# Second layer's modulation vector: computed by VectorE multiplies and short column sums in the dense rows instead of wide TensorE products before them

## The reference, cut to what matters

```
modulation(cvec, w_ada, b_ada) = split(silu(cvec) @ w_ada + b_ada, 6)      # w_ada[l] is 1024 x 6144
h = rmsnorm(x, norm1_g) * (1 + sc1) + sh1;  x = x + g1 * mixer(h)
h = rmsnorm(x, norm2_g) * (1 + sc2) + sh2;  x = x + g2 * channel(h)
```

## Time and profile before

| | |
|---|---|
| median of 3 runs | 1482.9 us (1482.24 to 1485.37) |
| the profiled execution | 1484.85 us, its span 1483.0 us |
| mean granted TensorE clock | 0.974 of full |
| busy: PE / PEld / DVE / ACT | 1384.1 / 821.8 / 525.7 / 398.7 us |
| chain that ended last, by engine | PE 77%, DMA 12%, DVE 6% |

### The profile page before, as it was taken

The page is one execution under the profiler, slowest core; times in us unless marked ns, Lnnn a source line. Parts: engine busy times, 40 slices in busy tenths (PEclk is TensorE's granted clock), DMA queues, the critical chain, the costliest instruction groups (busy, mean ns, idle before and its releaser), DMA issues.

```text
span 1483.0 us, 25756 instructions
## 1 busy us (share of the span) xinstructions
PE 1384.1 (93%) x11327; PEld 821.8 (55%) x11327; DVE 525.7 (35%) x954; ACT 398.7 (27%) x701; POOL 4.1 (0%) x8
## 2 busy tenths in 40 slices
PE   6899889999999999989898999999999998889886
PEld 3688657888888888878675343333333332223221
DVE  2799884523232333469864112011100010001022
ACT  3522485422222322376482111010110010000001
POOL 0000000000000000000000000000000000000010
PEclk9999899999999999999999999999999999999898
DMA  9997903532331052411418999999999999999995
GB/s 353 385 343 274 352 2 114 171 114 68 103 114 57 29 187 97 143 57 58 171 41 341 399 371 409 406 409 406 409 407 408 408 406 410 405 410 406 408 410 221
DMA packets 147031, 395.92 MB, mean 267 GB/s; under 512 B 7488, under 2 KB 38752, under 8 KB 146912
## 3 DMA queue, kind: packets, MB, share of 16 engines
q1 hardware_dynamic: 144000, 388.86, 68.7%
q10 hardware_dynamic: 2336, 3.24, 0.6%
q0 software_dynamic: 576, 2.10, 0.4%
HBM read 390.76 MB, written 3.41 MB: 266 GB/s over the span
## 4 chain that ended last, share of the span: by engine, by line
PE 77%; DMA 12%; DVE 6%; SPq 2%; ACT 2%; issue 1%; DVEq 0%; ACTq 0%
PE bank L1196 22%; DMA weight_ring<-in_exp_w 9%; PE bank L1154 8%; PE bank L1013 5%; PE bank L1014 5%; PE bank L1012 5%; PE bank L735 4%; PE bank L736 4%; PE bank L737 4%; DMA weight_ring<-in_w_ada 3%; PE bank L1021 3%; PE bank L1022 3%; PE bank L1023 3%; PE bank L1162 2%; PE bank L681 2%; DVE weight_ring L1865 2%
## 5 line engine op out<-in xcount | busy, mean ns | idle before, releaser
L1196 PE MATMUL bank<-weight_ring,gathered 128*32 128x512 f32 (+1 forms) x3840 | 402.2, 569 | 32.9 <-DMA weight_ring<-in_exp_w 27.1
L1196 PEld LDWEIGHTS bank<-weight_ring,gathered 128*32 128x32 f32 x3840 | 127.0, 112 | 283.0 <-issue 282.3
L2259 DVE TENSOR_TENSOR scratch<-scratch,bank 64x512 f32<-64x512 f32 (+1 forms) x60 | 38.4, 640 | 357.2 <-ACT scratch L1672 354.9
L1154 PE MATMUL bank<-weight_ring,scratch 128*32 128x512 f32 x1344 | 157.8, 593 | 2.2 <-DMA weight_ring<-in_exp_w 2.2
L1014 PE MATMUL bank<-slot_halves,slot_halves 128*128 128x512 f32 x336 | 130.9, 390 | 0.0
L1013 PE MATMUL bank<-hT_halves,slot_halves 128*128 128x512 f32 x336 | 130.9, 390 | 0.0
L1012 PE MATMUL bank<-slot_halves 128*128 128x512 f32 x320 | 124.8, 390 | 0.0
L1865 DVE SCALAR_TENSOR_TENSOR weight_ring<-scratch,conv_weights,weight_ring 128x512 f32<-128x512 f32 (+1 forms) x207 | 121.3, 637 | 2.6 <-ACT weight_ring L1453 0.7
L736 PE MATMUL bank<-hT_halves,slot_halves 128*128 128x512 f32 (+1 forms) x352 | 122.0, 347 | 0.0
L735 PE MATMUL bank<-slot_halves,slot_halves 128*128 128x512 f32 (+1 forms) x284 | 105.6, 372 | 8.1 <-DVE slot_halves L1772 5.2
L1154 PEld LDWEIGHTS bank<-weight_ring,scratch 128*32 128x32 f32 x1344 | 43.8, 110 | 100.3 <-issue 91.0
(11 more groups left out here) (303 smaller groups left out, 1576.1 us busy)
## 6 DMA issues: line engine op xcount, KB each, us to landing
weight_ring<-in_exp_w SPq DMA_DIRECT2D x216, 1024.0 KB, 18.5
weight_ring<-in_w_ada SPq DMA_DIRECT2D x24, 2048.0 KB, 13.5
weight_ring<-in_exp_w SPq DMA_DIRECT2D x64, 768.0 KB, 15.0
weight_ring<-in_ffn_w SPq DMA_DIRECT2D x33, 1024.0 KB, 5.4
weight_ring<-in_w_in SPq DMA_DIRECT2D x8, 1024.0 KB, 11.6
weight_ring<-in_w_out SPq DMA_DIRECT2D x4, 2048.0 KB, 11.2
weight_ring<-in_w_in SPq DMA_DIRECT2D x2, 3072.0 KB, 15.2
expert_rows<-scratch ACTq DMA_DIRECT2D x14, 128.0 KB, 6.0
```

Source lines behind the costliest of these rows:

```text
L1154: i = mm(bank[6][quarter, :], at01[:, c0:c0 + BLOCK], w2[:, i_, half * 512:(half + 1) * 512], start=(first and i_ == 0), stop=(last and i_ ...
L1196: i = mm(ps[BLOCK * job:BLOCK * (job + 1), 0:cw], gathered_block(e, k, b), w[:, kk, a * cw:(a + 1) * cw], start=(k == 0), stop=(k == KT - 1))
```

## The change

Layer 1's twelve pieces leave the walk. `modulate`, `turn_modulation`, `modulation_rows` and `modulation` for l = 1 go, and so do their 12 loads of 2 MB. Instead, from dense row 2 on, VectorE multiplies: each weight row k of a piece is scaled with the silu value of its partition and added into an accumulator of 128 x 512. A step is one such instruction; a piece of b = 0 has 16 (8 weight rows for two vectors), the others 8 (the latent vector alone), 128 steps in all. Eight steps go into each of rows 2 to 17, four behind each `piece_rest`. The weights come in halves of 1 MB into two buffers, 24 transfers on SP's queue, placed ahead of the loads of later weight groups. Two rows after a piece's last step, TensorE sums its accumulators over the partitions at the start of a row (`late_sums`): 8 matmuls for a piece of b = 0 and 4 for the others, of the form of L830. `late_modulation` adds the bias.

```diff
-MOD_PIECES = [(l, b, n) for l, b in MOD_TURNS for n in ([0, 3, 1, 2] if (l, b) == (1, 0) else range(4))]
+MOD_TURNS = [(0, 0), (0, 1), (0, 2)]
+MOD_PIECES = [(l, b, n) for l, b in MOD_TURNS for n in range(4)]
+LATE_PIECES = [(b, n) for b in range(3) for n in range(4)]
+LATE_ROW = 2
+        def late_place(piece, v):
+            return 2 * (piece % 2) + v if LATE_PIECES[piece][0] == 0 else piece % 4
+            def late_weights(i):
+                piece, half = divmod(i, 2)
+                b, n = LATE_PIECES[piece]
+                if i == 0:
+                    sp.wait_ge(L[0]["wo_mm"], KT)
+                if i >= 2:
+                    sp.wait_ge(late_step, STEPS_OF_HALF[i - 2])
+                sp.dma_start(late_w[i % 2], k_major(t["w_ada"][1], 512 * (4 * b + n), 512 * (4 * b + n + 1))[
+                    :, 4 * half:4 * half + 4, :]).then_inc(late_landed[i % 2], 16)
+            def late_sums(piece):
+                b, n = LATE_PIECES[piece]
+                pe.wait_ge(late_step, STEPS_OF_PIECE[piece])
+                for j in range(4):
+                    for v in range(2 if b == 0 else 1):
+                        at = 4 * (4 * n + j) + 2 * v
+                        i = mm(bank[LATE_BANK[b]][:, at:at + 2], late_acc[late_place(piece, v)][:, j * P:(j + 1) * P],
+                               const("ones")[:, 0:2], start=True, stop=True)
+                i.then_inc(mod_mm, 1)
-                    if l == 0 and i_ == 5:
-                        modulate(1, 2, 3)
-                        modulate(1, 1, 0)
-                        modulate(1, 1, 1)
...
-                if l == 0:
-                    modulate(1, 0, 0)
-                if l == 0:
-                    modulate(1, 0, 3)
                 norm_broadcast(3 * l + 3, TQ)
-                if l == 0:
-                    modulate(1, 0, 1)
-                    modulate(1, 0, 2)
-                        if n == 3:
-                            turn_modulation(1, 0)
                         if n >= 2:
                             pe.wait_ge(a_ready, n - 1)
+                        for done in range(len(LATE_PIECES)):
+                            if late_row_of(STEPS_OF_PIECE[done] - 1) + 2 == n:
+                                late_sums(done)
+            def late_steps_done(begin, end):
+                for s in range(begin, min(end, len(LATE_STEPS))):
+                    piece, half, k, v = LATE_STEPS[s]
+                    i = 2 * piece + half
+                    if s == 0 or LATE_STEPS[s - 1][0:2] != (piece, half):
+                        dve.wait_ge(late_landed[i % 2], 16 * (i // 2 + 1))
+                    if k == 0:
+                        held_by_piece = [q for q in range(piece) if late_place(q, 0) // 2 == late_place(piece, 0) // 2 or
+                                         LATE_PIECES[q][0] and late_place(q, 0) == late_place(piece, v)]
+                        if held_by_piece:
+                            dve.wait_ge(mod_mm, len(MOD_PIECES) + held_by_piece[-1] + 1)
+                        ts(dst, w, x, None, ALU.mult).then_inc(late_step, 1)
+                    else:
+                        dve.wait_ge(late_step, LATE_STEPS.index((piece, (k - 1) // 4, k - 1, v)) + 1)
+                        stt(out=dst, in0=w, scalar=x, in1=dst, op0=ALU.mult, op1=ALU.add).then_inc(late_step, 1)
                         if 0 < n < NF - 1:
                             piece_rest(2 * n + 2)
+                            if s >= 0:
+                                late_steps_done(s, s + 4)
...
                             piece_rest(2 * n + 3)
+                            if s >= 0:
+                                late_steps_done(s + 4, s + 8)
```

More of the change, by code:

```diff
@@ L36 @@
 RING = TAIL + 6 * D
-MOE0 = 56
+MOE0 = 44
 STAGE = SLOTS - 1
@@ L76, with late_steps, late_row_of @@
 SELECTS = len(GATHERS) + 1
+def late_steps():
+    steps = []
+    for piece, (b, n) in enumerate(LATE_PIECES):
+        for half in range(2):
+            for v in range(2 if b == 0 else 1):
+                for k in range(4):
+                    steps.append((piece, half, 4 * half + k, v))
+    order = []
+    for piece in range(len(LATE_PIECES)):
+        for half in range(2):
+            mine = [s for s in steps if s[0] == piece and s[1] == half]
+            order += sorted(mine, key=lambda s: (s[2], s[3]))
+    return order
+LATE_STEPS = late_steps()
+STEPS_OF_PIECE = [sum(s[0] <= piece for s in LATE_STEPS) for piece in range(len(LATE_PIECES))]
+STEPS_OF_HALF = [sum((s[0], s[1]) <= (i // 2, i % 2) for s in LATE_STEPS) for i in range(2 * len(LATE_PIECES))]
+def late_row_of(step):
+    return LATE_ROW + step // 8
 def unit_at(v):
@@ L261, in backbone @@
         mrow = [ring[:, OFF[2] + 4096 + i * 512:OFF[2] + 4608 + i * 512] for i in range(2)]
+        late_in = [ring[:, OFF[3] + 4096:OFF[3] + 6144], ring[:, TAIL + 4096:TAIL + 6144]]
+        late_w = [a.rearrange("p (k n) -> p k n", k=4) for a in late_in]
+        late_acc = [ring[:, OFF[2] + 4096 + i * 512:OFF[2] + 4608 + i * 512] for i in range(4)]
         conv_sq = [scr[:, 3584 + i * 512:4096 + i * 512] for i in range(NC)]
@@ L276, in backbone @@
                  "o_ready",
-                 "wo_mm", "x1", "sq2", "scaled2", "h2_ready"]
-        once = {n: sem(n) for n in ["norm_mm", "norm_inv", "norm_spread", "ks_mm", "ks_ready", "v_mm", "v_ready", "conv3", "mean_mm",
+                 "wo_mm", "x1", "scaled2", "h2_ready"]
+        once = {n: sem(n) for n in ["sq1", "sq2", "norm_mm", "norm_inv", "norm_spread", "ks_mm", "ks_ready", "v_mm", "v_ready", "conv3", "mean_mm",
                                  "u_sig", "sc_mm", "nb_ready", "pv_mm", "mix_ready", "qk_norm", "qk_rot", "cd_ready", "cd_mm",
@@ L311, in backbone @@
         eps_ready = sem("eps_ready")
+        late_landed = [sem(f"late_weights_{i}") for i in range(2)]
+        late_step = sem("late_step")
         def k_major(w, a, b):
@@ L360, in backbone @@
             ada(0, 2, n, [4, 2, 3][n % 3])
-        for n in range(8):
-            ada(1, 1 + n // 4, n % 4, [2, 3, 4][n % 3])
-            if n == 3:
-                out_projection(0, 0, 0)
+        out_projection(0, 0, 0)
         out_projection(0, 1, 1)
[L366 to L369, removed]
         F[0]["w13"] = [fill([(KT, 256, 0, k_major(t["ffn_w1"][0], 256 * g, 256 * g + 256)),
@@ L399, in backbone, with late_free_row, fill_free_row @@
             last[sl] = n
+        def late_free_row(i):
+            return late_row_of(STEPS_OF_HALF[i - 2] - 1) + 0.9 if i >= 2 else 0
+        def fill_free_row(group):
+            return 2 * (group - STAGE) + 2 if group >= STAGE else -1
         unit_base = [level[s] if s < SLOTS and third == 0 else 0 for s, third in RING_AT]
@@ L516, in fill_sums @@
             return sums(g - 1, 2 - spot % 2)
+        DONE_BEFORE = 3
+        LATE_BANK = [5, 6, 7] if (0, 0) in LATE_PIECES else [None, 4, 7]
+        def late_place(piece, v):
+            return 2 * (piece % 2) + v if LATE_PIECES[piece][0] == 0 else piece % 4
         FIRST_FILL_BANK = [7, 6, 5, 3]
@@ L557, in _ @@
             sp.dma_start(xtok[:, 2:4, :], t["ctx"][0].rearrange("(n p) d -> p n d", p=P)).then_inc(ctx_in, 16)
+            def late_weights(i):
[7 more added lines that the diff above has]
+                    :, 4 * half:4 * half + 4, :]).then_inc(late_landed[i % 2], 16)
+            late = iter(range(2 * len(LATE_PIECES)))
+            waiting = next(late)
             for n, (parts, free) in enumerate(fills):
+                group = (F[0]["w13"] + F[0]["w2"]).index(n) if n in F[0]["w13"] + F[0]["w2"] else None
+                while group is not None and waiting is not None and late_free_row(waiting) <= fill_free_row(group):
+                    late_weights(waiting)
+                    waiting = next(late, None)
                 if n >= SLOTS:
@@ L691, in turn_modulation, with norm_stat @@
                 i.then_inc(mod_t, 1)
-            def norm_stat(sq, src, k, T):
-                pe.wait_ge(sq, k + 1)
+            def norm_stat(sq, src, k, T, squares=0):
+                pe.wait_ge(sq, squares + k + 1)
                 for b in range(T // P):
@@ L881, in _ @@
                 if l == 0:
-                    pe.wait_ge(mod_row, 8)
+                    pe.wait_ge(mod_row, 6)
                 def score(p):
@@ L903, in _ @@
                         if l == 0:
-                            pe.wait_ge(mod_done, 5)
+                            pe.wait_ge(mod_done, 3)
                         else:
@@ L1535, in _ @@
                         modulation_rows(0, 2)
[L1536 to L1539, removed]
                     if l == 1:
@@ L1610, in _ @@
                 if l == 0:
[L1611 removed]
+                    act.wait_ge(mod_mm, 4 * 3)
                 shift(m, l, 1, "scaled2", "h2_ready")
@@ L1793, in modulation, with late_modulation, modulated @@
                 dve.wait_ge(mod_t, turn + 1)
+                ps = bank[7][:, :].rearrange("p (m q) -> p m q", q=32)[:, :, 0:2]
```

(27 more changed lines are left out.)

33 lines of the change are left out of this document (9 added, 24 removed).

## The result

The changed kernel takes 1496.33 us (median of 6 runs, 1494.52 to 1499.7), the kernel before 1482.87 (6 runs); the ratio is 1.0085, 95% interval 1.0074 to 1.0096, so 11.0 to 14.2 us slower. The prediction was 1493.9 us (+11.0), range 1487 to 1500. The profiled execution took 1494.66 us, its span is 1492.9. `rotate` is now L869, the taps L1937, the first score reduction L2024, a step of VectorE L1875 or L1878, `piece_rest` L1824, `late_sums` L774, `norm_broadcast` L763, the rows L1059 to L1061.

A forecast was written before the change was run, and what follows sets the result against it. TensorE was taken as full in walk and dense rows, VectorE nearly full in the walk. Terms -2.9 (walk), -1.3 (first spreading), +1.9 (second norm), -0.5 (turning), +13.8 (sums) gave +11.0: 1493.9 us, range 1487 to 1500.

The forecast's parts named there:

- Nothing gained up to `rotate(0)`: Walk: `rotate(0)` waits for VectorE's eleven taps, so 7.2 us of removed TensorE work turn into idle time.
- The walk gains 2.9: Walk behind `rotate(0)`: 5.0 us of VectorE time won, less 2.1 for the clock; bounds 2.2 to 5.0.
- A fall of the clock costs 2.1: Walk's tile 3 and second norm: TensorE idles, its clock halves, 2.1 us lost each time.
- The first spreading 1.3 earlier: First norm behind attention: without piece (1, 0, 0), L706 starts near 225.5 instead of 226.80, 1.3 us gained.
- The second norm loses 1.9: Second norm behind attention: uncovered TensorE gaps make the clock fall, 2.1 us lost against small gains, net 1.9.
- The sums cost 13.8: Dense rows: 64 small matmuls at 0.099 us a record, 12.6, plus 1.2 for slower wide products, all on TensorE's path.
- The turning saves 0.5: Dense row 3: the removed turning (1, 0) saves 0.5 us of TensorE.
- VectorE fits: Dense rows: 8.5 to 9.4 us of VectorE work a row costs TensorE nothing; 0.5 us spare in four tight rows.
- Nothing behind the dense part gives any of it back: Layer 1 after the dense rows: it and its transfers are released by earlier products, so no time is regained.
- The case with another sign: Walk: VectorE does not hold `rotate(0)`, all removed TensorE time reaches the end, 1470.9 us; chance 0.05.
- The case of cheap sums: Dense rows: sums cost like the removed pieces' records, 5.2 instead of 13.8 us, giving 1485.3 us; chance 0.08.
- The case of late accumulators: Rows 12, 14, 16, 18: held accumulators or late landings stop VectorE past its spare, +5 us, 1499; chance 0.12.

The follow-up runs named there:

- the filler in the walk: The changed kernel with seven products without use on TensorE ahead of `rotate(0)`: 1494.13 us, ratio 1.0070 to the kernel before.
- at the norm: The changed kernel with two useless products before the spreading of layer 0's second norm and three behind it: 1495.06 us, ratio 1.0075 to the kernel before.
- the turned sums: The changed kernel with 32 columns of ones loaded and the accumulator streaming, plus copies and transposes for four pieces: 1492.07 us, ratio 1.0051 to the kernel before.

## Why the prediction was right, point by point

- *Nothing gained up to `rotate(0)`*: right, 7.25 us of standing where 7.2 were worked out. *The walk gains 2.9*: 3.24. *A fall of the clock costs 2.1*: 1.9 by the filler in the walk, 1.6 at the norm, each inside the bounds of 1.1 and 2.8 (the upper one should be 2.9, as 648.50 to 654.3 is 5.8 us). TensorE worked 3.9 and 3.8 us at half clock there.
- *The first spreading 1.3 earlier*: 222.76 is 83.6 us behind `rotate(0)`, before 88.0; without the walk's 3.24 that is 1.2. *The second norm loses 1.9*: row 0 starts 0.1 us earlier by this place alone, its fall cost 1.6, net 1.5.
- *The sums cost 13.8*: this term was sized too small. The rows show 4 x 1.85 + 8 x 0.95 = 15.0, above the bound of 14.5 too. I took 0.099 a record from one group of eight, and it is not the price of one more: sixteen take 1.68 against 0.79, 0.111 for each record more, and 0.16 us goes beside what the group holds in the chain, 0.12 of it on the first wide product behind (0.35 for 0.23), where I took 0.1 in all.
- *The turning saves 0.5*: 10.88 for 11.37.
- *VectorE fits*: right, with 0.7 us to spare in the tight rows where 0.5 was worked out; it was busy 69% of rows 2 to 17, not near 80%. *Transfers cost nothing*: right, the bare rows take 10.88 us in both kernels.
- Sum of the measured terms: -3.2 - 1.2 + 1.5 - 0.5 + 15.0 = +11.6. The start of the second projection, 392.9 us behind `rotate(0)` against 381.3, is +11.6. The forecast of +11.0 came nearer than its terms, which is in part luck: up to row 0 they came to -2.9 where -2.3 was forecast, the sums cost 1.2 more than forecast, and the two misses have opposite signs.
- *Nothing behind the dense part gives any of it back*: not shown. From the second projection to the end the changed kernel's trace takes 960.8 us, that of the kernel before 962.9, so the two profiled executions are only 9.8 us apart. The nine traces spread from 960.8 to 963.3 us there, so the 2.1 can't be put down to the change either.
- The ratio's interval is 11.0 to 14.2 us, so the forecast lies at its lower edge. Whether the last us of the median's excess belongs to the change isn't settled: the changed kernel's runs spread over 5.2 us at mean clocks of 0.966 to 0.970, the shortest two at the highest, but no trace of one of the longest was taken.

The case with another sign was refuted where it was set: VectorE did hold `rotate(0)`. The case of cheap sums failed on the load; the turned sums come nearer to its price in another form (10 us in the rows, turnings included, where that case had 5.2). The case of late accumulators failed by 0.7 us.

## What to carry to other kernels

Work that fills an engine's waiting time can cost nothing, and taking it away may cost something: here the freed time became 7.25 us of idling and a lower clock. Before work is moved, ask of each piece what the engine would do instead at that place; the gain came from placing three pieces 2 to 4 us later (counted from `rotate(0)`), in another wait of the same engine. And a sum over partitions was cheaper here with the wide operand streaming (0.86 us a row) than with it loaded (1.85).

## What the runs showed of the hardware that I had not expected

- The clock can fall while TensorE is fully busy by its records: behind 3.47 us of 32 two-column products with full weight loads it went to half for 3.4 us, three times out of four, and not behind groups of 1.68 us.
- Sixteen records of the same sum take 1.84 us with 128 columns loaded for 2 and 0.67 with 32 loaded for 128.
- Steps of VectorE that each wait for the step before in their accumulator take 3.11 us for four in one accumulator (at 421.22) and 2.73 alternating between two (at 394.50): 0.78 and 0.68 each.
